# VectorE scales the attention exponentials, GpSimd makes the low halves of the 24 gate chunks, and the heads' low halves come three units later

## The chip, the cores and the metric

One program runs on one core of a Trainium2 chip. The metric is the time of an execution on the device in microseconds (us). The engines named below are TensorE (PE in the rows; PEld is its weight load), VectorE (DVE), ScalarE (ACT), GpSimd (POOL) and SyncE (SP), which issues most of the DMAs. Each engine works through its own queue in order, and the engines meet at semaphores.

## What is computed

The reference is one layer of a hybrid decoder trunk for 512 tokens of width 1024, in float32:

```python
h = rmsnorm(x, norm_mix_pre)
(a_q, a_kc, ..., b_q, ..., c_q, c_k, c_v, mg) = split(h @ w_in)
o_a = nsa_mixer(...)      # 8 heads of 64: compressed, selected and window attention, each with a softmax
o_b = gla_mixer(...)      # chunked gated linear attention
o_c = moba_mixer(...)     # 8 heads of 64: one softmax each
g = sigmoid(mg)           # 3 gates of 1024 channels for each token
merged = g0 * (o_a @ w_branch_a) + g1 * (o_b @ w_branch_b) + g2 * (o_c @ w_branch_c)
x = x + rmsnorm(merged @ w_out)
x = x + rmsnorm((silu(gate) * up) @ w_ffn_out)      # gate, up = split(rmsnorm(x) @ w_ffn_in)
```

In the stretch that is changed two things go on at once: the softmax attention of NSA's selected and window branches and of MoBA, and the products of the normed tokens with the `mg` columns of `w_in` (the gates).

## The kernel before, in words

**Weights.** All weights come from HBM as chunks of 128 x 1024 floats, in a fixed order. SyncE fetches chunk `c` into one of four raw slots (`fetch`, L816). ScalarE makes the high half, a rounded copy, with `hi(c)` (L1026, the activation is L1032). VectorE or GpSimd makes the low half, raw minus high, with a `lo(c)` of its own (VectorE: L1387, instruction L1391; GpSimd: L962, instruction L967). TensorE then takes three matmuls for each product: low x high, high x low, high x high (`three`, lines L2002, L2003, L2004). There are two slots for the halves (`SPLIT_SLOTS`), so `hi(c)` waits until the matmuls of chunk `c - 2` are done. `lo_split` (L371) is the wait for a low half: it picks the semaphore of VectorE or of GpSimd by the chunk's number. Before the change GpSimd makes the chunks from `N_EARLY` to `C_MERGE - 1`, which are those of the input projections, and VectorE makes all others: among them the 24 gate chunks, `C_GATE` to `C_BR - 1`.

**Attention.** It is one loop of 110 steps (`STEPS`), written out on each engine in the same order. A unit is one tile of 128 queries of one pass; there are 24 passes (two for each of the 8 NSA heads, one for each of the 8 MoBA heads) with four units each, 96 in all. The tiles of a pass go 3, 2, 1, 0, so a unit has 512, 384, 256 and 128 keys in turn (causal). In step `u`

- TensorE (`attention_pe`, L745) makes the scores of unit `u` (L761, L762), transposes scaled exponentials for `v = u - 6` (L770; it waits for `s_prob`), multiplies the transposed values of `v = u - 8` with V (L785, L787; it waits for `t_lo`), and then does a quarter of a gate chunk: six matmuls of 512 columns. A gate chunk `f` is used in the steps `4f` to `4f + 3`.
- VectorE (`attention_dve`, L639) adds the bias and takes the row maximum of unit `u` (L654; `s_max`). When `u` is a multiple of 4 it takes the reciprocals of the four row sums of the pass before (L672 for MoBA, L675 and L676 with the NSA gate; `s_rcp`). It makes the low half of the transposed values for `v = u - 7` (L681; `t_lo`), adds the two halves of a finished head (L687; `head_sum`) in steps with `u % 4 == 1`, and makes a gate chunk's low half in steps with `u % 4 == 2`. In the first unit of a head it also writes the far bias of the next head (L510).
- ScalarE (`attention_act`, L548) takes the exponentials of unit `u` with their row sum (L554), the high half of the transposed values for `v = u - 6` (L563), copies half of a finished head (L570) and its high half (L577; `head_hi`), and in steps with `u % 4 == 1` copies the finished gate logits out (L584) and makes the high half of the next gate chunk (L1032).
- GpSimd (L993) multiplies the exponentials of unit `u` in place with the reciprocal (`scale`, L970, instruction L974; `s_prob`), and makes the low half of a finished head (`head_low`, L976, instruction L979; `head_lo`) eight units after the head's last unit.

A head's low half is waited for by ScalarE two heads later (L569) and by TensorE where the branch products start (L725, L737). The first two gate chunks are made ahead of this: `C_GATE` by VectorE in its loop over the projections (L1703), `C_GATE + 1` in step 1 (L658).

Of the kernel before, what the change touches and what calls it, by code (L numbers as in the profile page):

```python
# [22 lines left out]
ALU = mybir.AluOpType  # L23
# [3 lines left out]
P = 128  # L27
# [21 lines left out]
C_MERGE = len(STRAIGHT)  # L49
N_GATES = 3 * KD  # L50
C_GATE = C_MERGE
C_BR = C_GATE + N_GATES
# [18 lines left out]
NX_OF = {k: (j, k - ks[0]) for j, ks in enumerate(NX_K) for k in ks}  # L71
N_FIRST = len(NX_K) + 1
N_EARLY = len(NX_K) + 12
C_POOL = C_MERGE - N_EARLY
FIRST_MOBA = STRAIGHT.index(("cq", 0))
CMP_BACK = FIRST_MOBA + 4

# [45 lines left out]
UNITS = [(br, n, i) for br, n in PASSES for i in TILE_ORDER]  # L123
# [6 lines left out]
def head_units(n):  # L130
    return (8 * n, 8 * n + 7) if n < 8 else (N_NSA + 4 * (n - 8), N_NSA + 4 * (n - 8) + 3)
# [3 lines left out]
LAST_OF = {head_units(n)[1]: n for n in range(N_HEADS)}  # L135
# [19 lines left out]
def count(c):  # L155

    return c - N_SEVEN if c >= C_FOUT else c


def program(nc, wpack, small_d, rows_d, mask_d, x_d, xt_d, pre_d, out_d):  # L160
    ctx = ExitStack()
    with ctx:
        def sem(name):
            return ctx.enter_context(nc.semaphore(name))
# [143 lines left out]
        w_lo_pool, w_lo_dve = sem("w_lo_pool"), sem("w_lo_dve")  # L308
# [35 lines left out]
        s_rcp, s_prob, t_full, pv_done = sem("s_rcp"), sem("s_prob"), sem("t_full"), sem("pv_done")  # L344
# [26 lines left out]
        def lo_split(eng, c):  # L371
            if c < N_EARLY:
                eng.wait_ge(w_lo_dve, c + 1)
            elif c < C_MERGE:
                eng.wait_ge(w_lo_pool, c + 1 - N_EARLY)
            else:
                eng.wait_ge(w_lo_dve, count(c) + 1 - C_POOL)

# [30 lines left out]
        def split_weights(c):  # L409

            return extra.get(c) or (wh[:, c % SPLIT_SLOTS, :], wl[:, c % SPLIT_SLOTS, :])
# [69 lines left out]
        def head_column(n):  # L481

            return 4 * (n % 2) + n // 2 if n < 8 else n
# [14 lines left out]
        def probs(u):  # L498

            i = UNITS[u][2]  # L500
            return sc[:, u // 4 % 3, P_AT[i]:P_AT[i] + P * (i + 1)]

        def stat_of(u, k):
            i = UNITS[u][2]
            return ast[:, u // 4 % 3, k, i:i + 1]

        def far_bias(eng, n):

            h = head_column(n)
            eng.tensor_copy(fullb[:, n % 2, 0:256], small[:, S_FAR + h:S_FAR + h + 1].broadcast_to([P, 256])).then_inc(bias_far, 1)  # L510

        def score_bank(u):
            return bank[u % 2]
# [4 lines left out]
        def output_bank(n):  # L518
            return bank[4 + n % 2]

        def head_rows(n):

            b = 64 * (n % 2)
            o = (oa if n < 8 else oc)[b:b + 64, n % 8 // 2, :, :]
            return tmp[b:b + 64, :], o[:, 0, :], o[:, 1, :]
# [113 lines left out]
        def attention_dve(ve, link, lo, stacked_low):  # L639
            ve.wait_ge(ob_out, 32)  # L640
            ve.wait_ge(near_out, 32)
            for u in range(STEPS):
                if u < len(UNITS):
                    k = UNITS[u][1]
                    n = P * (UNITS[u][2] + 1)
                    ve.wait_ge(s_full, u + 1)
                    if u % 4 == 0 and u >= 12:

                        ve.wait_ge(t_full, u - 8)
                    if u in FIRST_OF:  # L650
                        ve.wait_ge(bias_far, k + 1)
                        ve.wait_ge(band_in[k % 2], 16 * (k // 2 + 1))

                    ve.tensor_tensor_reduce(probs(u), score_bank(u)[:, 0:n], fullb[:, k % 2, 512 - n:512],  # L654
                                            -1.0, 3e38, ALU.add, ALU.min, stat_of(u, 0)).then_inc(s_max, 1)
                    if u == 0:
                        stacked_low(C_MERGE - 1)
                    if u == 1:  # L658
                        lo(C_GATE + 1)
                    if u in FIRST_OF and 1 <= k < N_HEADS - 1:  # L660

                        ve.wait_ge(s_max, u)
                        far_bias(ve, k + 1)
                H = u // 4 - 1
                if u % 4 == 0 and 0 <= H < len(PASSES):
                    br, n = PASSES[H]
                    mine = ast[:, H % 3, :, :]
                    ve.wait_ge(s_exp, 4 * H + 4)
                    if H >= 3:
                        ve.wait_ge(s_prob, 4 * (H - 2))  # L670
                    if br == "m":
                        ve.reciprocal(mine[:, 2, :], mine[:, 1, :]).then_inc(s_rcp, 1)  # L672
                    else:
                        g = 3 * head_column(n) + (1 if br == "s" else 2)
                        link(ve.reciprocal(mine[:, 3, :], mine[:, 1, :]))  # L675
                        ve.tensor_tensor(mine[:, 2, :], mine[:, 3, :], gate[:, :, g], ALU.mult).then_inc(s_rcp, 1)  # L676
                v = u - T_LAG - 1
                if 0 <= v < len(UNITS):
                    n = P * (v % 4 + 1)
                    ve.wait_ge(t_hi, v + 1)  # L680
                    ve.tensor_tensor(ptl[v % 3][:, 0:n], bank[2 + v % 2][:, 0:n], pth[v % 3][:, 0:n].bitcast(F32),  # L681
                                     ALU.subtract).then_inc(t_lo, 1)
                n = LAST_OF.get(u - PV_LAG - 2)
                if n is not None:
                    part = head_rows(n)[0]
                    ve.wait_ge(head_part, n + 1)
                    ve.tensor_tensor(part, output_bank(n)[0:64, :], part, ALU.add).then_inc(head_sum, 1)  # L687
                if u % 4 == 2 and 0 <= u // 4 - 1 < N_GATES + 2:
                    lo(C_GATE + u // 4 + 1)

        def compressed_scores_pe(te, mm):
# [248 lines left out]
        def _(pool):  # L940
# [21 lines left out]
            def lo(c):  # L962
                s, b = c % RAW_SLOTS, c % SPLIT_SLOTS
                n = width_of(c)
                landed(pool, s, c // RAW_SLOTS)
                pool.wait_ge(w_hi, c + 1)
                pool.tensor_tensor(wl[:, b, 0:n], raw[:, s, 0:n], wh[:, b, 0:n].bitcast(F32),  # L967
                                   ALU.subtract).then_inc(w_lo_pool, 1)

            def scale(u):  # L970

                n = P * (UNITS[u][2] + 1)
                pool.wait_ge(s_rcp, u // 4 + 1)
                pool.tensor_tensor(probs(u), probs(u), stat_of(u, 2).broadcast_to([P, n]), ALU.mult).then_inc(s_prob, 1)  # L974

            def head_low(n):  # L976
                part, hi_, lo_ = head_rows(n)
                pool.wait_ge(head_hi, n + 1)
                pool.tensor_tensor(lo_, part, hi_.bitcast(F32), ALU.subtract).then_inc(head_lo, 1)  # L979

            for c in range(C_MERGE):
                if N_EARLY <= c + 2 < C_MERGE:
                    lo(c + 2)
                if c == 6:
                    pool.wait_ge(h_lo, KD)
                    pool.memset(state[:, :, :, :], 0.0).then_inc(const_ready, 1)
                k = c - C_O
                if 0 <= k < NT:
                    pool.wait_ge(o_ms, k + 1)
                    pool.tensor_tensor(stat[:, 32 + 4 * k:36 + 4 * k], stat[:, 16 + 4 * k:20 + 4 * k],  # L990
                                       minus_half[:, 0:4], ALU.pow).then_inc(o_rstd, 1)

            for u in range(len(UNITS) + 8):  # L993
                if u < len(UNITS):
                    scale(u)
                n = LAST_OF.get(u - 8)
                if n is not None:
                    pool.wait_ge(s_prob, min(u + 1, len(UNITS)))
                    head_low(n)
                    pool.wait_ge(head_lo, n + 1)  # L1000
            def y_power(t):
# [350 lines left out]
        def _(ve):  # L1352
# [34 lines left out]
            def lo(c):  # L1387
                high, low = split_weights(c)
                ve.wait_ge(w_hi, count(c) + 1)
                n = width_of(c)  # L1390
                ve.tensor_tensor(low[:, 0:n], raw[:, c % RAW_SLOTS, 0:n], high[:, 0:n].bitcast(F32),  # L1391
                                 ALU.subtract).then_inc(w_lo_dve, 1)
# [120 lines left out]
            for c in range(C_MERGE):  # L1513
# [185 lines left out]
                if c == FIRST_MOBA + 2:  # L1699
                    ve.wait_ge(cmp_ready, 7)  # L1700
                    far_bias(ve, 0)
                    far_bias(ve, 1)
                if c + 2 == C_MERGE:  # L1703
                    lo(c + 2)
            attention_dve(ve, link, lo, stacked_low)

            for s in range(N_GATES):
                n, b = PRODUCTS[s]
# [237 lines left out]
            with ve.Fori(0, 4) as i:  # L1946
                for k in range(4, 8):
                    c = C_FOUT + k
# [48 lines left out]
        def _(te):  # L1997
# [391 lines left out]
            with te.Fori(0, 4) as i:  # L2389
                for k in range(2, 6):  # L2390
                    te.wait_ge(w_hi, i * 4 + count(C_FOUT + k) + 1)
                    te.wait_ge(w_lo_dve, i * 4 + count(C_FOUT + k) + 1 - C_POOL)
                    te.wait_ge(a_hi, i * 4 + k + 1)
# [123 lines left out]
```

## Time and profile before

| | |
|---|---|
| median of 3 runs | 924.05 us (923.48 to 928.54) |
| the profiled execution's own time | 925.45 us |
| its span, first to last instruction | 923.7 us |
| mean granted TensorE clock | 0.997 |
| TensorE busy | 915.4 us (99%) |
| TensorE weight load busy | 806.4 us (87%) |
| VectorE busy | 594.7 us (64%) |
| ScalarE busy | 471.3 us (51%) |
| GpSimd busy | 158.7 us (17%) |
| first and last score matmul of attention | 237.6 us and 452.0 us after the start |

The span is that of the profiled execution; its own time is 1.75 us more, which lies around the span. In the rows below, times are in us from the span's start, "mean ns of one" is an instruction's mean duration, and the idle time at a row's end is that of the engine just before the instruction, with what ended it. Instructions of one engine overlap at their edges: the next one starts some 0.06 us before the one in front of it has ended.

### The profile page before, as it was taken

The page shows a single profiled execution, that of the slowest core. Times are in us where ns is not written, and L with a number is a line of the kernel's source. Part 1 is how long each engine was busy: PE and PEld are TensorE (multiplying, and loading weights), DVE is VectorE, ACT ScalarE, POOL GpSimd, SP SyncE. Part 2 cuts the span into 40 slices and gives each one's busy share as a digit, 9 for nine tenths or more (in the row PEclk, how much of TensorE's full clock was granted, in tenths as well). Part 3 has the DMA queues.
Part 4 walks back from the last instruction along what each step waited for, and adds up shares of the span by engine and source line. Part 5 has one row for each costly group of instructions (what it writes and reads, how often), then busy time and mean ns, then how long its engine had stood idle before and what let it go on. Part 6 is the DMA issues. An engine that isn't in the chain of part 4 may idle for free.

```text
span 923.7 us, 14517 instructions
## 1 busy us (share of the span) xinstructions
PE 915.4 (99%) x5287; PEld 806.4 (87%) x5287; DVE 594.7 (64%) x1146; ACT 471.3 (51%) x912; POOL 158.7 (17%) x168
## 2 busy tenths in 40 slices
PE   9999999999999999999999999999999999999997
PEld 8888888888888888888888888989999999988886
DVE  5998665462555555556667758778888888533335
ACT  6743245333566656676754445255555555323232
POOL 3000263344133334343410001000000000000000
PEclk9999999999999999999999999999999999999999
DMA  9323627222323232464246751122232233232222
GB/s 347 121 71 87 197 92 228 69 92 92 108 81 103 88 102 87 124 246 149 82 170 251 263 166 63 47 92 92 101 128 93 93 110 120 99 107 91 91 91 91
DMA packets 37726, 113.62 MB, mean 123 GB/s; under 512 B 4452, under 2 KB 7076, under 8 KB 36908
## 3 DMA queue, kind: packets, MB, share of 16 engines
q1 hardware_dynamic: 36828, 109.08, 34.7%
q10 hardware_dynamic: 832, 3.67, 1.3%
q8 instruction: 40, 0.66, 0.3%
q14 instruction: 26, 0.21, 0.1%
HBM read 98.87 MB, written 13.66 MB: 122 GB/s over the span
## 4 chain that ended last, share of the span: by engine, by line
PE 98%; DVE 1%; DMA 1%; SPq 0%; issue 0%; ACT 0%; DVEq 0%
PE bank L2002 28%; PE bank L2003 27%; PE bank L2004 27%; PE bank L770 3%; PE bank L762 2%; PE bank L787 2%; PE bank L785 2%; PE bank L761 1%; PE bank L2066 1%; PE bank L2021 1%; DMA xT<-x_features 1%; PE bank L2195 0%; PE bank L2253 0%; PE bank L701 0%; PE bank L2116 0%; PE bank L2182 0%
## 5 line engine op out<-in xcount | busy, mean ns | idle before, releaser
L1032 ACT ACTIVATE w_hi<-w_raw 128x1024 fp32r<-128x1024 f32 (+1 forms) x84 | 88.5, 1054 | 129.1 <-PE bank L2004 125.4
L2002 PE MATMUL bank<-h_hi,w_lo 128*128 128x512 f32 x352 | 140.5, 399 | 0.0
L2003 PE MATMUL bank<-h_lo,w_hi 128*128 128x512 f32 x352 | 138.2, 393 | 0.0
L2004 PE MATMUL bank<-h_hi,w_hi 128*128 128x512 f32 x352 | 138.0, 392 | 0.0
L1391 DVE TENSOR_TENSOR w_lo<-w_raw,w_hi 128x1024 fp32r<-128x1024 f32 (+2 forms) x63 | 77.0, 1223 | 40.7 <-ACT w_hi L1032 40.5
L654 DVE CUSTOM_DVE_ANT_0 sc<-bank,fullb 128x512 f32<-128x512 f32 (+1 forms) x96 | 47.0, 489 | 77.8 <-PE bank L762 76.0
L554 ACT ACTIVATE sc<-sc,ast 128x512 f32<-128x512 f32 (+1 forms) x96 | 53.9, 561 | 72.8 <-DVE ast L654 72.8
L974 POOL TENSOR_TENSOR sc<-sc,ast 128x512 f32<-128x512 f32 (+1 forms) x96 | 66.2, 720 | 130.8 <-DVE ast L676 97.8
L2003 PE MATMUL bank<-tx_lo,op_hi 128*128 128x256 f32 x288 | 81.5, 283 | 0.0
L2004 PE MATMUL bank<-tx_hi,op_hi 128*128 128x256 f32 x288 | 81.5, 283 | 0.0
L2002 PE MATMUL bank<-tx_hi,op_lo 128*128 128x256 f32 x288 | 81.5, 283 | 0.0
L2004 PEld LDWEIGHTS bank<-h_hi,w_hi 128*128 128x128 f32 x352 | 66.5, 189 | 14.6
L2002 PEld LDWEIGHTS bank<-h_hi,w_lo 128*128 128x128 f32 x352 | 66.6, 189 | 11.4
L2003 PEld LDWEIGHTS bank<-h_lo,w_hi 128*128 128x128 f32 x352 | 66.6, 189 | 11.3
L967 POOL TENSOR_TENSOR w_lo<-w_raw,w_hi 128x1024 fp32r<-128x1024 f32 x22 | 52.7, 2397 | 114.7 <-ACT w_hi L1032 114.7
L1834 DVE TENSOR_TENSOR op_lo<-op_sum,op_hi 128x512 fp32r<-128x512 f32 x72 | 49.5, 687 | 20.5 <-ACT op_hi L1270 19.9
L2002 PE MATMUL bank<-w_hi,as_lo 128*128 128x512 f32 x160 | 62.3, 389 | 0.0
L2003 PE MATMUL bank<-w_lo,as_hi 128*128 128x512 f32 x160 | 62.3, 389 | 0.0
L2004 PE MATMUL bank<-w_hi,as_hi 128*128 128x512 f32 x160 | 62.2, 389 | 0.0
L2003 PE MATMUL bank<-h_lo,op_hi 128*128 128x256 f32 x216 | 61.1, 283 | 0.0
L2004 PE MATMUL bank<-h_hi,op_hi 128*128 128x256 f32 x216 | 61.1, 283 | 0.0
L2002 PE MATMUL bank<-h_hi,op_lo 128*128 128x256 f32 x216 | 61.1, 283 | 0.0
(360 smaller groups left out, 2308.8 us busy)
## 6 DMA issues: line engine op xcount, KB each, us to landing
w_raw<-wpack SPq DMA_DIRECT2D x144, 512.0 KB, 3.6
gate_logits<-gl_out SPq DMA_DIRECT2D x24, 256.0 KB, 2.2
gl_in<-gate_logits SPq DMA_DIRECT2D x24, 256.0 KB, 5.3
near_bias<-near_bias ACTq DMA_DIRECT2D x1, 2880.0 KB, 13.4
xT<-x_features SPq DMA_DIRECT2D x8, 256.0 KB, 5.8
xs<-x_in SPq DMA_DIRECT2D x4, 512.0 KB, 8.8
fullb<-near_bias SPq DMA_DIRECT2D x16, 128.0 KB, 2.9
ckx<-cks SPq DMA_DIRECT2D x16, 128.0 KB, 2.8
```

What stands on the lines that cost most here:

```text
L554: sa.activation(probs(u), probs(u), ACT.Exp, bias=stat_of(u, 0), scale=-1.0, accum_out=stat_of(u, 1)).then_inc(s_exp, 1)
L654: ve.tensor_tensor_reduce(probs(u), score_bank(u)[:, 0:n], fullb[:, k % 2, 512 - n:512], -1.0, 3e38, ALU.add, ALU.min, stat_of(u, 0)).then ...
L762: mm(score_bank(u)[:, 0:m], query(n)[:, cols], k1[:, 0:m], start=False, stop=True).then_inc(s_full, 1)
L770: last = te.transpose(bank[2 + v % 2][:, P * (i - j):P * (i - j) + P], sc[:, H % 3, P_AT[i] + P * j:P_AT[i] + P * j + P], ident[:, :])
L967: pool.tensor_tensor(wl[:, b, 0:n], raw[:, s, 0:n], wh[:, b, 0:n].bitcast(F32), ALU.subtract).then_inc(w_lo_pool, 1)
L974: pool.tensor_tensor(probs(u), probs(u), stat_of(u, 2).broadcast_to([P, n]), ALU.mult).then_inc(s_prob, 1)
L1032: sa.activation(split_weights(c)[0][:, 0:n], raw[:, s, 0:n], ACT.Copy).then_inc(w_hi, 1)
L1391: ve.tensor_tensor(low[:, 0:n], raw[:, c % RAW_SLOTS, 0:n], high[:, 0:n].bitcast(F32), ALU.subtract).then_inc(w_lo_dve, 1)
L1834: ve.tensor_tensor(opl[o % RING][:, :], source, oph[o % RING][:, :].bitcast(F32), ALU.subtract).then_inc(op_lo, 1)
L2002: mm(out, ll, rh, start=start, stop=False, skip_group_check=True)
L2003: mm(out, lh, rl, start=False, stop=False, skip_group_check=True)
L2004: return mm(out, lh, rh, start=False, stop=stop, skip_group_check=True)
```

## The change

GpSimd's `scale` goes away. In step `u` VectorE now multiplies the exponentials of unit `u - 4` in place with a `tensor_scalar` whose scalar is a column of one value per partition; it does so after the reciprocals and ahead of the low half of the transposed values. GpSimd makes the low halves of all 24 gate chunks: the first two at the end of its loop over the projections, the others in steps with `u % 4 == 2`, the place that VectorE had for them. VectorE keeps the chunks from `C_BR` on. A head's low half follows on GpSimd 11 units after the head's last unit, in place of 8, right behind a gate chunk's low half and a wait for it. No DMA is added, removed or moved.

```diff
-C_POOL = C_MERGE - N_EARLY
+C_POOL = C_BR - N_EARLY
...
         def lo_split(eng, c):
             if c < N_EARLY:
                 eng.wait_ge(w_lo_dve, c + 1)
-            elif c < C_MERGE:
+            elif c < C_BR:
                 eng.wait_ge(w_lo_pool, c + 1 - N_EARLY)
             else:
                 eng.wait_ge(w_lo_dve, count(c) + 1 - C_POOL)
...
                     if u == 0:
                         stacked_low(C_MERGE - 1)
-                    if u == 1:
-                        lo(C_GATE + 1)
...
                         ve.tensor_tensor(mine[:, 2, :], mine[:, 3, :], gate[:, :, g], ALU.mult).then_inc(s_rcp, 1)
+                v = u - 4
+                if 0 <= v < len(UNITS):
+                    ve.wait_ge(s_rcp, v // 4 + 1)
+                    ve.tensor_scalar(probs(v), probs(v), stat_of(v, 2), None, ALU.mult).then_inc(s_prob, 1)
                 v = u - T_LAG - 1
...
-                if u % 4 == 2 and 0 <= u // 4 - 1 < N_GATES + 2:
+                if u % 4 == 2 and N_GATES <= u // 4 + 1 < N_GATES + 4:
                     lo(C_GATE + u // 4 + 1)
...
-            def scale(u):
-
-                n = P * (UNITS[u][2] + 1)
-                pool.wait_ge(s_rcp, u // 4 + 1)
-                pool.tensor_tensor(probs(u), probs(u), stat_of(u, 2).broadcast_to([P, n]), ALU.mult).then_inc(s_prob, 1)
-
...
             for c in range(C_MERGE):
-                if N_EARLY <= c + 2 < C_MERGE:
+                if N_EARLY <= c + 2:
                     lo(c + 2)
...
-            for u in range(len(UNITS) + 8):
-                if u < len(UNITS):
-                    scale(u)
-                n = LAST_OF.get(u - 8)
+            for u in range(len(UNITS) + 12):
+                if u % 4 == 2 and 2 <= u // 4 + 1 < N_GATES:
+                    lo(C_GATE + u // 4 + 1)
+                n = LAST_OF.get(u - 11)
                 if n is not None:
-                    pool.wait_ge(s_prob, min(u + 1, len(UNITS)))
+                    pool.wait_ge(w_lo_pool, min(C_GATE + u // 4 + 1, C_BR - 1) + 1 - N_EARLY)
                     head_low(n)
                     pool.wait_ge(head_lo, n + 1)
...
-                if c + 2 == C_MERGE:
-                    lo(c + 2)
             attention_dve(ve, link, lo, stacked_low)
```

## Rows read from the trace of the kernel before

**Rows 1.** Page, the chain that ended last, shares of the span by engine.
```profile
PE 98%; DVE 1%; DMA 1%; SPq 0%; issue 0%; ACT 0%; DVEq 0%
```

**Rows 2.** Busy time of one stretch of attention: stretch, length, then each engine's busy us.
```profile
251.50:442.00 190.50, 190.50 (x1044) 164.27 (x1043) 111.74 (x331) 124.41 (x314) 72.48 (x96) 1.00 0.37 121
```

**Rows 3.** Groups by line: count | busy us, mean ns of one | idle before.
```profile
L1391 DVE TENSOR_TENSOR w_lo<-w_raw,w_hi 128x1024 fp32r<-128x1024 f32 x27 | 33.6, 1245 | 15.0 <-ACT w_hi L1032 15.0
...
L681 DVE TENSOR_TENSOR pTl<-bank,pTh 128x384 fp32r<-128x384 f32 x24 | 13.3, 553 | 2.3 <-ACT pTh L563 2.3
...
L681 DVE TENSOR_TENSOR pTl<-bank,pTh 128x128 fp32r<-128x128 f32 x24 | 6.8, 285 | 0.0
...
L974 POOL TENSOR_TENSOR sc<-sc,ast 128x512 f32<-128x512 f32 (+1 forms) x96 | 66.2, 720 | 130.8 <-DVE ast L676 97.8 <-DVE ast L672 33.0
L967 POOL TENSOR_TENSOR w_lo<-w_raw,w_hi 128x1024 fp32r<-128x1024 f32 x22 | 52.7, 2397 | 114.7 <-ACT w_hi L1032 114.7
```

**Rows 4.** Groups by line, VectorE operations with one SBUF input and an SBUF output.
```profile
L1412 DVE COPY rb<-stat 128x512 f32<-128x512 f32 x1 | 0.4, 428 | 0.9 <-POOL stat L960 0.9
...
L1666 DVE TENSOR_SCALAR ghid<-ghid 64x128 f32<-64x128 f32 x1 | 0.2, 220 | 0.0
```

**Rows 5.** Timeline, around gate chunk 7 (kind C): start us, duration us, instruction.
```profile
292.48 0.69 DVE L687 TENSOR_TENSOR tmp<-bank,tmp 64x512 f32<-64x512 f32 x1
...
293.37 0.63 ACT L577 ACTIVATE oa<-tmp 64x512 fp32r<-64x512 f32 x1
...
294.64 1.06 ACT L1032 ACTIVATE w_hi<-w_raw 128x1024 fp32r<-128x1024 f32 x1
...
295.39 0.28 PE L762 MATMUL bank<-ak,aqs 128*128 128x128 f32 x1
...
295.74 1.23 DVE L1391 TENSOR_TENSOR w_lo<-w_raw,w_hi 128x1024 fp32r<-128x1024 f32 x1 [0.99 <-ACT w_hi L1032]
...
298.29 0.19 PEld L785 LDWEIGHTS bank<-pTh,av 128*128 128x128 f32 x1
...
298.51 0.19 PEld L2002 LDWEIGHTS bank<-h_hi,w_lo 128*128 128x128 f32 x1
```

**Rows 6.** Timeline, high halves of gate chunks 5, 22 (kind B) and 23 (C), chunk 5's use.
```profile
275.74 1.05 ACT L1032 ACTIVATE w_hi<-w_raw 128x1024 fp32r<-128x1024 f32 x1
...
280.02 0.19 PEld L2002 LDWEIGHTS bank<-h_hi,w_lo 128*128 128x128 f32 x1
...
432.59 1.05 ACT L1032 ACTIVATE w_hi<-w_raw 128x1024 fp32r<-128x1024 f32 x1
...
442.13 1.06 ACT L1032 ACTIVATE w_hi<-w_raw 128x1024 fp32r<-128x1024 f32 x1
```

**Rows 7.** Timeline, GpSimd behind ScalarE in the projections.
```profile
227.00 1.06 ACT L1032 ACTIVATE w_hi<-w_raw 128x1024 fp32r<-128x1024 f32 x1 [3.28 <-PE bank L2004]
...
228.20 2.39 POOL L967 TENSOR_TENSOR w_lo<-w_raw,w_hi 128x1024 fp32r<-128x1024 f32 x1 [3.04 <-ACT w_hi L1032]
```

**Rows 8.** Timeline, a small VectorE operation with and without a low half on GpSimd.
```profile
125.88 0.17 DVE L1641 TENSOR_SCALAR stat<-stat 128x4 f32<-128x4 f32 x1
...
127.11 2.37 POOL L967 TENSOR_TENSOR w_lo<-w_raw,w_hi 128x1024 fp32r<-128x1024 f32 x1
...
128.93 0.57 DVE L1641 TENSOR_SCALAR stat<-stat 128x4 f32<-128x4 f32 x1
```

**Rows 9.** Timeline, gate chunk 2 early in attention.
```profile
248.56 1.05 ACT L1032 ACTIVATE w_hi<-w_raw 128x1024 fp32r<-128x1024 f32 x1
...
252.16 0.30 PE L785 MATMUL bank<-pTh,av 128*128 128x128 f32 x1
```

**Rows 10.** Timeline, a MoBA head's first unit behind chunk 19 (kind C).
```profile
405.60 1.06 ACT L1032 ACTIVATE w_hi<-w_raw 128x1024 fp32r<-128x1024 f32 x1
...
409.85 0.29 DVE L510 COPY fullb<-small 128x256 f32<-128x256 f32 x1
...
411.66 0.36 PE L785 MATMUL bank<-pTh,cv 128*128 128x256 f32 x1
```

## The prediction

> **What bounds the kernel now.** I read the chain that ended last first: 98% of it is TensorE [rows 1]. Then the busy time by stretch: over 190.5 us of attention TensorE is busy for 190.50 us, at a granted clock of 1.00, while VectorE has 111.74 us of work, ScalarE 124.41 and GpSimd 72.48 [rows 2]. The list of waits has none of TensorE's inside attention. So nothing that the change takes off VectorE, ScalarE or GpSimd can make attention shorter: the steps already follow each other at TensorE's own pace. What is left to ask is whether one of the changed results comes later than TensorE asks for it. For that I read the timeline, gate chunk by gate chunk.
>
> **The change part by part.**
>
> *Scales leave GpSimd.* 96 instructions of 720 ns, 69.1 us, all beside TensorE's work [rows 3]; gain 0.
>
> *Low halves come to GpSimd.* 24 of 2.397 us, 57.5 us, in place of 24 of 1.245 us (29.9 us) on VectorE [rows 3]. GpSimd's load falls by 11.6 us, but each low half is ready later. GpSimd starts 0.14 us after the high half's end (227.00 + 1.06 = 228.06, start 228.20) [rows 7], VectorE 0.04 us after it [rows 5].
>
> *Scales come to VectorE.* No row shows this operation with a column as its scalar. The nearest, one SBUF input and an SBUF output, take 220 ns for 128 elements and 428 ns for 512 [rows 4], so 0.54 ns an element: 0.22, 0.29, 0.36 and 0.43 us, 1.30 for a pass and 31.1 us in all, against the 29.9 that leave. The lower bound is these; the upper is one element a cycle, 285 ns for 128 and 553 for 384 [rows 3]. I take the lower. VectorE is 59% busy in this stretch, so the sum costs nothing; its place in the queue can. The Trainium skill ("VectorE: DVE Perf Modes", section on the TRN2 errata) gives 58 cycles plus half the elements at 0.96 GHz. An estimate by it is 0.26 us for 384 elements; the rows of this case say 0.36, and the sum would stay at its size by either.
>
> *What stands behind a scale on VectorE.* In steps with u % 4 == 1 the scale of 384 stands ahead of L681 and of L687, which come 0.30 us later (0.36 less the overlap of 0.06). In the passes in which a head ends, ScalarE's L577 waits for L687. L687 then ends at 292.48 + 0.69 + 0.30 = 293.47, L577 starts at 293.52 in place of 293.37 [rows 5], and the high half behind it on ScalarE comes 0.15 us later.
>
> *When the low halves are ready.* The 24 chunks fall in three kinds. A (9 chunks, no head ends) has over 1.2 us in hand. B (chunks 5, 9, 13, 17, 20, 22; first and last high half in [rows 6]): 275.74 + 1.05 + 0.15 + 0.14 + 2.40 = 279.48, and TensorE loads it at 280.02: 0.54 us in hand. C (chunks 7, 11, 15, 19, 21, 23; first in [rows 5], last in [rows 6]): 294.64 + 1.06 + 0.15 + 0.14 + 2.40 = 298.39, loaded at 298.51: 0.12 us in hand. So the gate matmuls just don't wait.
>
> *The shared access.* L1641, 128 x 4, takes 0.17 us by itself; where a low half is running on GpSimd it takes 0.57 and ends at 129.50, while the low half ends at 129.48 [rows 8]. VectorE was held until GpSimd's instruction was over. The new scale is an operation of this kind, and the 128-wide one (u % 4 == 3) falls into GpSimd's low half. Behind it in VectorE's queue stands L681 for 128 elements, for which TensorE's L785 waits in the next step. It would end 0.31 us behind GpSimd's low half (0.03 + 0.28).
> The Trainium skill ("Advanced Engine Details and Errata", VectorE Performance Modes) says that two-port VectorE instructions and GpSimd's block each other. Rows 8 show VectorE's side alone. An estimate by the other side: GpSimd's low half would start up to 0.2 us later in kind C, and the gates would wait some 0.1 us there, 0.6 us in all.
>
> - A: over 0.9 us in hand, 0.
> - B: 279.48 + 0.31 = 279.79, needed at 280.02 - 0.22 = 279.80; with 0.05 for the semaphore, 0.05 us each, 0.3 us.
> - C: it is a race. VectorE's L654 can start at 295.39 + 0.28 = 295.67 and the scale 0.21 later, at 295.88; GpSimd starts at 294.64 + 1.06 + 0.15 + 0.14 = 295.99. If VectorE is in first, 0. If GpSimd is, L681 ends at 298.70 and is needed at 298.29 [rows 5]: 0.4 us each. Bounds 0 and 2.4 us; the two starts are within 0.11 us, so I take half, 1.2.
> - Chunk 2, before the pipeline is full: 248.56 + 1.05 + 0.14 + 2.40 + 0.31 = 252.46, needed at 252.13 [rows 9]: 0.35 us once.
>
> *Heads' low halves.* They move behind a gate chunk's low half, so to 409.45 to 410.74 in [rows 10] (405.60 + 1.06 + 0.15 + 0.14 + 2.40, and 0.1 for the wait on its own semaphore). Those who wait for them do so two heads later, or, for the last head, behind a high half whose time doesn't move: 0. But VectorE's L510 (409.85) is of the held kind too. Held to 410.87, with the reciprocal, the scale of 512 and L681 for 256 behind it, VectorE is ready near 411.8, and L785 wants it at 411.66: 0.2 us in the three MoBA chunks of kind C, 0.6 us, less what has been lost there already (0.3). In NSA's passes the reciprocals' product is held so, with 0.04 us or nothing at the end.
>
> *Queues.* SyncE's fetch of chunk c + 4 waits for chunk c's low half, four steps after it is made; nothing moves. TensorE's waits keep their number.
>
> Sum: 0.3 + 1.2 + 0.35 + 0.3 = 2.15, rounded to 2.0 us longer. The profiled execution has 925.45 us; so 927.45 against it. The median of the runs is 1.40 us below it: 924.05 + 2.0 = 926.0 us, +0.2%. About 0.5% (4.6 us) is what a measurement of this kernel can tell from no change.
>
> **The rivals.**
>
> *Nothing moves.* VectorE wins every race and the 0.05 us are not there: 924 us. For it: TensorE's steps have the same length to a few ns from pass to pass. Against it: chunk 2's margin is negative by my rows.
>
> *The hold goes on through the head's low half.* Slower than before clearly. In the 12 passes of kinds B and C GpSimd has the head's low half (1.29 us) right behind the chunk's. If VectorE's waiting scale doesn't get in between, L681 for 128 is late by a further 1.39 us: B 1.4 us, C 1.8, so 6 x 1.4 + 6 x 1.8 = 19 us, 943 us. It decides in the gap between the two GpSimd instructions. Against it: GpSimd waits there for its own semaphore, and in rows 8 VectorE went on within 0.02 us.
>
> *Scale at one element a cycle.* Then it isn't of the two-port kind and (as the reductions beside GpSimd in the trace) isn't held; but L687 is 0.5 us later, the high half 0.35, and the gates of kind C wait 0.1 to 0.2 us: 925 us.
>
> *A gain.* It would need a wait of TensorE that the profile doesn't show. A faster VectorE frees ScalarE's exponentials by 0.1 to 1 us in steps with u % 4 == 3, but TensorE asks for them two steps later.
>
> **How the numbers follow.** The forecast (waits of some tenths in few passes, +0.5 to +4 us) 0.60; nothing moves 0.16; one element a cycle 0.06; held through both 0.09; more stalls of the forecast's kind than I counted, over 4.6 us, 0.06; a gain over 0.5% 0.03. Slower by over 0.5%: 0.09 + 0.06 = 0.15, with a little of the forecast's tail 0.17. Faster 0.03. The rest, 0.80, is within 0.5%. The range starts at 923.3, a little under no change, and ends at 930, where all races are lost (+3.9) and two tenths more are lost in each pass of kind B or C.
>
> **What would show it.** Right: TensorE's waits in attention name L681 and are under 0.5 us each; TENSOR_SCALAR of 128 elements shows a mean near 1 us with an end at the end of GpSimd's L967, while that of 256 and 512 stays at 0.29 and 0.43; L967 has 46 instructions of 2.4 us. Wrong: idle of TensorE before L2002 by L967 (the low half itself is late), scales held over L979, or attention's length unchanged to 0.1 us.

## The result, and the profile after

The changed kernel takes 932.66 us (median of 7 runs, 930.68 to 934.01), against 924.16 us for the kernel before (median of 7, 923.48 to 928.54): 1.0086 times as long, with an interval of 1.0072 to 1.0099. So it is slower by 0.9%, outside the range of the prediction. The profiled execution of after took 932.66 us with a span of 930.9 us, 7.2 us more than the span of before. Both have the same mean granted clock (0.997).

The page of after: busy times, the chain that ended last, and two groups.

```profile
PE 918.7 (99%) x5287; PEld 805.2 (86%) x5287; DVE 630.0 (68%) x1218; ACT 471.5 (51%) x912; POOL 150.2 (16%) x96
...
PE 95%; DVE 2%; issue 1%; DMA 1%; SPq 0%; ACT 0%; DVEq 0%
...
L969 POOL TENSOR_TENSOR w_lo<-w_raw,w_hi 128x1024 fp32r<-128x1024 f32 x46 | 110.5, 2402 | 263.9 <-ACT w_hi L1028 263.9
...
L678 DVE TENSOR_SCALAR sc<-sc,ast 128x512 f32<-128x512 f32 (+1 forms) x96 | 66.1, 688 | 0.9
```

TensorE's share of the chain is 95%, where it was 98% [rows 1]. The low halves on GpSimd are what was forecast, 46 of 2.4 us. The scales on VectorE (L678) are not: 66.1 us in place of the 31.1 of the prediction, 688 ns each. The windows show where the time went (stretch, length, then the busy us of TensorE, its weight load, VectorE, ScalarE and GpSimd, the granted clock, and DMA), the stretch of [rows 2] in after:

```profile
251.50:442.00 190.50, 187.11 (x1008) 157.36 (x1007) 139.82 (x380) 120.07 (x302) 61.19 (x31) 1.00 0.36 118
```

TensorE was busy for all of these 190.50 us before; now it is idle for 3.39 us of them, at the same granted clock. (The ends of matmuls are modelled, so part of a wait can lie inside a busy time; the lengths of the steps, below, show all of it.) The groups by shape, in attention alone, say which scale is dear:

```profile
L678 DVE TENSOR_SCALAR sc<-sc,ast 128x128 f32<-128x128 f32 x24 | 34.4, 1435 | 0.0
...
L678 DVE TENSOR_SCALAR sc<-sc,ast 128x512 f32<-128x512 f32 x24 | 12.2, 510 | 0.8
...
L678 DVE TENSOR_SCALAR sc<-sc,ast 128x384 f32<-128x384 f32 x24 | 10.0, 417 | 0.0
L678 DVE TENSOR_SCALAR sc<-sc,ast 128x256 f32<-128x256 f32 x24 | 9.4, 391 | 0.0
```

The smallest takes longest: 1435 ns on average. It is the one that falls into GpSimd's low half; in 19 of the 24 passes it is held, for 1.33 to 2.47 us, and in five it takes 0.28. And the waits of TensorE in attention (from 237 to 480 us; us in total, times, longest), of which before had none there:

```profile
PEld bank L772 <- DVE sc L678: 7.1, 10, 0.9
...
PE bank L772 <- DVE pTl L683: 3.5, 7, 0.5
...
PEld bank L772 <- issue: 2.9, 11, 0.6
```

All stand at L772, the transposes, and not at the product with V (L787), where the prediction had looked. (One wait can stand both at the weight load and at the matmul, so the rows don't add up. The first names the scale, L678, which is not what they wait for. The transposes of step u ask for the scale of unit u - 6 and for the low half of unit u - 8. In the step of chunk 7 below, the scale that they ask for, of 256, had ended at 295.45, 4 us earlier; what they lack is the low half, L683.)

**Step by step.** Attention's first 95 steps, each taken from its first score matmul to that of the next, add up to 6.71 us more than in before. Attention starts 0.18 us earlier than in before, and 0.70 us more come behind the last score matmul: 0.63 of them are one more wait at the transposes (459.29, 0.80 us behind that matmul, where before has 0.17), behind a scale of 256 that a head's low half holds for 1.33 us. By the prediction's terms:

| place | measured, us | forecast, us |
|---|---|---|
| chunk 2 | 0.69 | 0.35 |
| kind B (chunks 5, 9, 13, 17; 20 and 22 nothing) | 0.26, 0.32, 0.28, 0.27 | 0.3 for six |
| kind C in NSA, u % 4 == 0 (chunks 7, 11, 15) | 0.69, 0.71, 0.66 | 1.2 for all six |
| kind C in MoBA, u % 4 == 1 (chunks 19, 21, 23) | 0.74, 0.71, 0.25 | 0.3 |
| first passes of seven NSA heads, u % 4 == 1 | 0.10 to 0.13 each, 0.82 in all | 0 |
| all other steps | 0.3 | 0 |

Chunk 7 shows the mechanism, in the timeline of after (start, duration, instruction):

```profile
295.72 1.06 ACT L1028 ACTIVATE w_hi<-w_raw 128x1024 fp32r<-128x1024 f32 x1
...
296.43 0.28 PE L764 MATMUL bank<-ak,aqs 128*128 128x128 f32 x1
...
296.92 2.41 POOL L969 TENSOR_TENSOR w_lo<-w_raw,w_hi 128x1024 fp32r<-128x1024 f32 x1 [8.19 <-ACT w_hi L1028]
...
296.96 2.45 DVE L678 TENSOR_SCALAR sc<-sc,ast 128x128 f32<-128x128 f32 x1
...
298.64 0.39 PE L763 MATMUL bank<-ak,aqs 128*128 128x512 f32 x1
...
299.33 0.28 DVE L683 TENSOR_TENSOR pTl<-bank,pTh 128x128 fp32r<-128x128 f32 x1
299.40 1.28 POOL L975 TENSOR_TENSOR oa<-tmp,oa 64x512 fp32r<-64x512 f32 x1
...
299.72 0.31 PEld L772 LDWEIGHTS bank<-ident,sc 128*128 128x128 f32 x3 [0.89 <-DVE sc L678]
299.75 0.52 PE L772 MATMUL bank<-ident,sc 128*128 128x128 f32 x3 [0.49 <-DVE pTl L683]
...
300.34 0.36 DVE L674 TENSOR_TENSOR ast<-ast,gate 128x4 f32<-128x4 f32 x1
...
301.72 0.34 PE L763 MATMUL bank<-ak,aqs 128*128 128x384 f32 x1
```

GpSimd is in first by 0.04 us. VectorE's scale of 128 then takes 2.45 us in place of 0.28 and ends at 299.41, 0.08 us behind GpSimd's end at 299.33. L683 behind it is done at 299.61, and TensorE's transposes have waited for it: the step from 298.64 to 301.72 is 3.08 us long. In before the same step takes 2.39 us, from 297.61 to 300.00, and its deadline stands in these rows of the timeline:

```profile
297.61 0.39 PE L761 MATMUL bank<-ak,aqs 128*128 128x512 f32 x1
...
298.07 0.49 PE L770 MATMUL bank<-ident,sc 128*128 128x128 f32 x3
...
298.29 0.19 PEld L785 LDWEIGHTS bank<-pTh,av 128*128 128x128 f32 x1
...
300.00 0.33 PE L761 MATMUL bank<-ak,aqs 128*128 128x384 f32 x1
```

The transposes of unit u - 6 overwrite the bank that was read for the low half of unit u - 8, so they wait for the same value of `t_lo` as the product with V of unit u - 8, and they stand ahead of it in TensorE's queue, 0.22 us earlier (298.29 - 298.07), or 0.36 us in steps with u % 4 == 1.

In MoBA VectorE wins the race (chunk 19, after), and pays later:

```profile
411.62 0.28 DVE L678 TENSOR_SCALAR sc<-sc,ast 128x128 f32<-128x128 f32 x1
411.68 2.48 POOL L969 TENSOR_TENSOR w_lo<-w_raw,w_hi 128x1024 fp32r<-128x1024 f32 x1 [8.21 <-ACT w_hi L1028]
...
414.23 1.30 POOL L975 TENSOR_TENSOR oa<-tmp,oa 64x512 fp32r<-64x512 f32 x1
...
414.57 1.11 DVE L510 COPY fullb<-small 128x256 f32<-128x256 f32 x1
...
415.80 0.49 DVE L678 TENSOR_SCALAR sc<-sc,ast 128x512 f32<-128x512 f32 x1
...
416.20 0.42 DVE L683 TENSOR_TENSOR pTl<-bank,pTh 128x256 fp32r<-128x256 f32 x1
...
416.76 0.63 PE L772 MATMUL bank<-ident,sc 128*128 128x128 f32 x4 [0.54 <-DVE pTl L683]
```

The far bias of the next head (L510, 0.29 us before [rows 10]) is held by the head's low half that the change puts here. With the reciprocal and the scale of 512 behind it, L683 is late for TensorE by 0.54 us.

### The profile page after: what moved, and what is told of

It reads as the page before. It is cut to its first block, busy times and chain, and to the rows that moved or that the text cites. A ratio compares the mean times of both kernels' runs of the same rounds, so it can differ in the third digit from the quotient of the medians.

```text
span 930.9 us, 14528 instructions
## 1 busy us (share of the span) xinstructions
PE 918.7 (99%) x5287; PEld 805.2 (86%) x5287; DVE 630.0 (68%) x1218; ACT 471.5 (51%) x912; POOL 150.2 (16%) x96
## 4 chain that ended last, share of the span: by engine, by line
PE 95%; DVE 2%; issue 1%; DMA 1%; SPq 0%; ACT 0%; DVEq 0%
PE bank L1996 27%; PE bank L1998 27%; PE bank L1997 27%; PE bank L772 3%; PE bank L789 2%; PE bank L764 2%; PE bank L787 1%; PE bank L2060 1%; PE bank L763 1%; PE bank L2015 1%; DMA xT<-x_features 1%; PE bank L2189 0%; DVE sc L678 0%; PE bank L2247 0%; PE bank L703 0%
## 5 line engine op out<-in xcount | busy, mean ns | idle before, releaser
L1028 ACT ACTIVATE w_hi<-w_raw 128x1024 fp32r<-128x1024 f32 (+1 forms) x84 | 88.4, 1054 | 129.3 <-PE bank L1998 125.7
L969 POOL TENSOR_TENSOR w_lo<-w_raw,w_hi 128x1024 fp32r<-128x1024 f32 x46 | 110.5, 2402 | 263.9 <-ACT w_hi L1028 263.9
L1996 PE MATMUL bank<-h_hi,w_lo 128*128 128x512 f32 x352 | 140.7, 400 | 0.0
L654 DVE CUSTOM_DVE_ANT_0 sc<-bank,fullb 128x512 f32<-128x512 f32 (+1 forms) x96 | 47.1, 490 | 60.1 <-PE bank L764 56.6
L1996 PE MATMUL bank<-tx_hi,op_lo 128*128 128x256 f32 x288 | 81.5, 283 | 0.0
L1996 PEld LDWEIGHTS bank<-h_hi,w_lo 128*128 128x128 f32 x352 | 66.6, 189 | 11.4
L1387 DVE TENSOR_TENSOR w_lo<-w_raw,w_hi 128x1024 fp32r<-128x1024 f32 (+2 forms) x39 | 47.6, 1221 | 29.9 <-ACT w_hi L1028 29.5
L678 DVE TENSOR_SCALAR sc<-sc,ast 128x512 f32<-128x512 f32 (+1 forms) x96 | 66.1, 688 | 0.9
L1996 PE MATMUL bank<-w_hi,as_lo 128*128 128x512 f32 x160 | 62.3, 389 | 0.0
L1996 PE MATMUL bank<-h_hi,op_lo 128*128 128x256 f32 x216 | 61.1, 283 | 0.0
```

Of the source, the lines that this page charges most:

```text
L678: ve.tensor_scalar(probs(v), probs(v), stat_of(v, 2), None, ALU.mult).then_inc(s_prob, 1)
L1028: sa.activation(split_weights(c)[0][:, 0:n], raw[:, s, 0:n], ACT.Copy).then_inc(w_hi, 1)
L1996: mm(out, ll, rh, start=start, stop=False, skip_group_check=True)
```

## The experiments

Line numbers move by a few between the kernels: the waits of TensorE below are always at its transposes. Each kernel is set against runs of the kernel before on the same chip; the sums "in attention" are taken step by step against before, as above.

**The scale behind the transposed low half.**

```diff
-                v = u - 4
-                if 0 <= v < len(UNITS):
-                    ve.wait_ge(s_rcp, v // 4 + 1)
-                    ve.tensor_scalar(probs(v), probs(v), stat_of(v, 2), None, ALU.mult).then_inc(s_prob, 1)
                 v = u - T_LAG - 1
...
                                      ALU.subtract).then_inc(t_lo, 1)
+                v = u - 4
+                if 0 <= v < len(UNITS):
+                    ve.wait_ge(s_rcp, v // 4 + 1)
+                    ve.tensor_scalar(probs(v), probs(v), stat_of(v, 2), None, ALU.mult).then_inc(s_prob, 1)
```

> The changed kernel with two lines of VectorE's queue exchanged: in every step the low half of the transposed values comes first, the scale second. Same work on every engine. Theory H (GpSimd's low half holds VectorE's two-port scale, and what stands behind the scale comes late): TensorE waits for the low half of the transposed values, which now stands ahead of the held scale, while the scale itself is asked for two steps later. So the waits of 0.26 to 0.71 us in the steps with u % 4 == 0 (4.1 us in all) vanish, and most of those of 0.1 to 0.74 in the steps with u % 4 == 1 (2.4 us) with them: 925 to 927 us; the 128-wide scales still last 1.4 us on average. Rival L (VectorE simply has more to do than its slack allows, scales of 0.28 to 0.49 us being dearer than forecast): its work is the same, so it stays late in sum, and the time stays at 930 us or more.

Measured: 924.39 us, 1.0000 times before (0.9990 to 1.0009); 0.31 us more in attention, all of it in two steps behind chunks 19 and 21. The whole 8 us are gone although the scale of 128 takes as long as before the exchange, 1422 ns on average where after has 1435. The time is 0.6 us below what was expected. The group by shape and the timeline at chunk 7:

```profile
L684 DVE TENSOR_SCALAR sc<-sc,ast 128x128 f32<-128x128 f32 x24 | 34.1, 1422 | 0.0
```

```profile
294.21 2.40 POOL L969 TENSOR_TENSOR w_lo<-w_raw,w_hi 128x1024 fp32r<-128x1024 f32 x1 [8.11 <-ACT w_hi L1028]
294.76 0.29 DVE L679 TENSOR_TENSOR pTl<-bank,pTh 128x128 fp32r<-128x128 f32 x1 [0.54 <-ACT pTh L563]
294.97 1.74 DVE L684 TENSOR_SCALAR sc<-sc,ast 128x128 f32<-128x128 f32 x1
...
296.28 0.49 PE L772 MATMUL bank<-ident,sc 128*128 128x128 f32 x3
```

The scale is held as before, to 296.71. But the low half of the transposed values (L679), which reads a PSUM bank, runs beside GpSimd in its 0.29 us and is done at 295.05, 1.2 us before TensorE asks for it. So what costs time is not the hold by itself, nor VectorE's load, but what is queued behind the scale, held or not.

**The scales alone** (low halves of the gate chunks stay on VectorE; heads' low halves after 11 units, without the wait for a gate chunk).

```diff
-C_POOL = C_BR - N_EARLY
+C_POOL = C_MERGE - N_EARLY
...
+                    if u == 1:
+                        lo(C_GATE + 1)
...
-                if u % 4 == 2 and 2 <= u // 4 + 1 < N_GATES:
-                    lo(C_GATE + u // 4 + 1)
```

> Only the scales move to VectorE; VectorE keeps the low halves of the gate chunks, and GpSimd has only the heads' low halves, 11 units behind a head. H: nothing long runs on GpSimd any more, so the 128-wide scale lasts 0.28 us; the heads' low halves run right behind ScalarE's high half and can hold the 256-wide scale of that step by up to 1.2 us, with the 512-wide low half of the transposed values behind it: up to 0.5 us in each of 12 passes that end a head. 925 to 931 us, with no wait in the steps u % 4 == 0 in which no head's low half runs. L: VectorE has 30 us more work in attention than in the changed kernel, so it is later everywhere: over 935 us.

Measured: 929.26 us, 1.0054 (1.0037 to 1.0071); 3.63 us in attention. The scale of 128 has 282 ns now, with no low half beside it. But 2.69 us come in four steps (u = 19, 35, 51, 67; 0.64 to 0.70 each), not in twelve passes as expected: at the other heads' low halves in attention VectorE's scale of 256 is in first. Timeline at u = 18 and 19:

```profile
273.68 1.28 POOL L977 TENSOR_TENSOR oa<-tmp,oa 64x512 fp32r<-64x512 f32 x1 [45.09 <-ACT oa L577]
...
273.76 1.36 DVE L680 TENSOR_SCALAR sc<-sc,ast 128x256 f32<-128x256 f32 x1
...
275.04 0.68 DVE L685 TENSOR_TENSOR pTl<-bank,pTh 128x512 fp32r<-128x512 f32 x1
...
275.87 0.41 PE L774 MATMUL bank<-ident,sc 128*128 128x128 f32 x2 [0.50 <-DVE pTl L685]
```

It is the same mechanism at another place: the head's low half now starts as soon as its high half is there, in the step whose scale is 256 wide, and holds that one. Another 1.04 us are in the first passes of the NSA heads (eight steps, 0.09 to 0.15 each; all other steps together are 0.1 us shorter), where GpSimd has nothing to do: there the queue is just too long for TensorE's transposes, as the reciprocals' product and the scale of 512 stand ahead of the low half.

**The low halves alone** (GpSimd keeps the scales, and takes the gate chunks too: four scales at the start of a pass, then the low half).

```diff
-                    ve.tensor_scalar(probs(v), probs(v), stat_of(v, 2), None, ALU.mult).then_inc(s_prob, 1)
...
+                if u % 4 == 0 and 4 <= u <= len(UNITS):
+                    for v in range(u - 4, u):
+                        scale(v)
                 if u % 4 == 2 and 2 <= u // 4 + 1 < N_GATES:
                     lo(C_GATE + u // 4 + 1)
...
+                    pool.wait_ge(s_prob, min(4 * (u // 4), len(UNITS)))
                     head_low(n)
```

> Only the low halves move: GpSimd makes the gate chunks' low halves and also scales, as it did before (four scales of a pass in a row, ahead of the next chunk's low half). VectorE has less work than in either kernel. H: VectorE has no two-port scale to be held; the far-bias copy can still be held by a head's low half, and the scales of a pass come behind that, 1 us later than before, with over 1 us in hand: 924 to 926 us. L: the same, 924 to 925. A third theory, that the GpSimd low halves themselves are late for the gate matmuls: waits in front of the gate matmuls in the kind-C chunks, 925 to 929.

Measured: 924.11 us, 1.0002 (0.9991 to 1.0012), and in attention 0.00 us: every step has its length of before, with 24 low halves of 2.4 us on GpSimd. So the low halves themselves are not late for the gates; they do harm only through what they hold.

**Heads' low halves back at 8 units.**

```diff
-            for u in range(len(UNITS) + 12):
+            for u in range(len(UNITS) + 8):
...
-                n = LAST_OF.get(u - 11)
+                n = LAST_OF.get(u - 8)
```

> The changed kernel with the third part undone: heads' low halves 8 units behind the head, so in GpSimd's queue ahead of the gate chunk's low half instead of behind it. H: the copy and the 512-wide scale in the steps u % 4 == 0 of the next pass are no longer held (the 2.4 us of waits in steps u % 4 == 1 vanish), but the head's low half (1.29 us) now runs while the 256-wide scale of step u % 4 == 2 wants the port: it is held by some 1.1 us, the low half of the transposed values behind it ends 0.65 us too late, in the 12 passes in which a head ends: +7.8 - 2.4, 936 to 939 us. L: GpSimd's order does not matter to VectorE: 932 to 933 us.

Measured: 932.16 us, 1.0084 (1.0067 to 1.0101); 7.48 us in attention. The three dear MoBA steps are gone (0.69 us are left in steps with u % 4 == 1, where after has 2.44), and the same four steps as with the scales alone come in, 0.70 to 0.74 each, 2.81 in all. The steps with u % 4 == 0 stay at 3.85 us in sum (4.06 in after), but not in place: chunks 5, 9, 13 and 17 now cost nothing, and chunks 20 and 22 cost 0.41 and 0.47. The 256-wide scales in this kernel:

```profile
L678 DVE TENSOR_SCALAR sc<-sc,ast 128x256 f32<-128x256 f32 x24 | 12.7, 530 | 0.0
```

I had expected twelve of these 24 to be held, and 936 to 939 us; four are, for 1.41 to 1.45 us, and the others take 0.35. Elsewhere VectorE is in first. The "three units later" of the change is therefore worth little by itself, 0.77 us in attention (7.48 against 6.71) and nothing in the medians: it trades one held instruction for another.

**The gate chunk's low half in two instructions of 512 columns.**

```diff
+                if c >= C_GATE:
+                    pool.tensor_tensor(wl[:, b, 0:512], raw[:, s, 0:512], wh[:, b, 0:512].bitcast(F32), ALU.subtract)
+                    pool.tensor_tensor(wl[:, b, 512:n], raw[:, s, 512:n], wh[:, b, 512:n].bitcast(F32),
+                                       ALU.subtract).then_inc(w_lo_pool, 1)
...
```

> The changed kernel, but GpSimd makes each gate chunk's low half in two instructions of 512 columns, back to back, with no semaphore between them. H with a grant between two GpSimd instructions: the held 128-wide scale lasts at most about 1.4 us (mean near 0.8 in place of 1.43) and the waits of 0.26 to 0.71 us in the steps u % 4 == 0 vanish; the two halves end some 0.2 us later than one instruction, so some kind-C gate matmuls may wait 0.2 us: 928 to 930 us. If VectorE is held through back-to-back instructions: scale mean 1.6 us and more, 933 to 936 us. L: no change, 932.

Measured: 931.68 us, 1.0090 (1.0073 to 1.0107); 5.07 us in attention. For the steps that the edit aims at the expectation holds: the scale of 128 falls to 749 ns, and 4.06 us at u % 4 == 0 become 0.52. VectorE gets in between two GpSimd instructions that stand back to back, with no semaphore between them. The total misses, since VectorE is now early for the next GpSimd instruction, the head's low half (timeline, chunk 7):

```profile
297.01 1.29 POOL L980 TENSOR_TENSOR oa<-tmp,oa 64x512 fp32r<-64x512 f32 x1
...
297.63 0.70 DVE L674 TENSOR_TENSOR ast<-ast,gate 128x4 f32<-128x4 f32 x1
...
299.33 0.52 PE L772 MATMUL bank<-ident,sc 128*128 128x128 f32 x3 [0.28 <-DVE pTl L683]
```

The product of 128 x 4, 0.17 us by itself, is held for 0.70, and the step with u % 4 == 1 pays 0.47 to 0.50 us in chunks 7, 11 and 15. The two dearest steps of MoBA stay (0.71 and 0.73).

**A constant in place of the column.** (This kernel leaves the normalisation of the exponentials out. Its instructions and waits are otherwise the same.)

```diff
-                    ve.tensor_scalar(probs(v), probs(v), stat_of(v, 2), None, ALU.mult).then_inc(s_prob, 1)
+                    ve.tensor_scalar(probs(v), probs(v), 0.5, None, ALU.mult).then_inc(s_prob, 1)
```

> The changed kernel with the scale's per-partition column replaced by the constant 0.5 (so the exponentials are not normalised; the waits are the same). It prices the column: if it costs the extra 0.06 us, the scales not held last 0.22, 0.29, 0.36 and 0.43 us, as the nearest rows of before had it, in place of 0.28, 0.35, 0.42 and 0.49. TensorE's waits then shrink by some 0.06 us each, 24 of them: 1 to 2 us less than the changed kernel.

Measured in one run: 931.26 us, 5.74 us in attention. The groups by shape:

```profile
L678 DVE TENSOR_SCALAR sc<-sc 128x128 f32<-128x128 f32 x24 | 34.1, 1420 | 0.0
...
L678 DVE TENSOR_SCALAR sc<-sc 128x384 f32<-128x384 f32 x24 | 8.5, 355 | 0.0
```

The 384-wide scale, which nothing holds, takes 355 ns with a constant and 417 ns with a column: 0.06 us is the price of the column. The held one doesn't change. The extra time in the first passes of the seven NSA heads falls from 0.82 us to 0.44 (0.05 to 0.09 each). In all, attention takes 0.97 us less than in after.

**Only the scales of 128, and only those of 512, behind the low half.** The edit of the first experiment for `v % 4 == 3` alone, and then for `v % 4 == 0` alone. The first of the two:

```diff
-                if 0 <= v < len(UNITS):
+                if 0 <= v < len(UNITS) and v % 4 < 3:
...
+                if 0 <= v < len(UNITS) and v % 4 == 3:
```

> The changed kernel; of the four scales of a pass only the 128-wide one (step u % 4 == 3, the one that GpSimd's low half of the gate chunk holds) goes behind the low half of the transposed values. H: the 4.1 us of waits in steps u % 4 == 0 vanish; those in steps u % 4 == 1 (2.4 us: copy and 512-wide scale) stay, or grow where VectorE no longer loses time before: 927.5 to 929.5 us. L: the order of one short scale changes the work of no step, 931 us or more.

> The changed kernel; only the 512-wide scale (step u % 4 == 0, beside the far-bias copy and the reciprocals) goes behind the low half of the transposed values. The 2.4 us of waits in steps u % 4 == 1 vanish, but for up to 0.2 us where the copy is held by a head's low half; the 4.1 us in steps u % 4 == 0 stay: 929 to 931 us. Together with the run before, the two parts are to add up to the whole of the first experiment. Of the 2.4 us the part in front of which no GpSimd instruction runs (0.1 us in each of 8 NSA heads' first passes, about 1 us) is plain queue length: the scale of 0.49 us in front of the low half of the transposed values.

Measured: 929.25 us (1.0062, 1.0045 to 1.0079) with the 128 behind: all of u % 4 == 0 is gone (4.06 to 0.00), and u % 4 == 1 costs 3.71. With the 512 behind, 927.61 us (1.0042, 1.0026 to 1.0059), below the 929 to 931 that were expected: u % 4 == 1 is all but gone (2.44 to 0.30), and u % 4 == 0 costs 3.23 in place of staying at 4.06. There chunks 5, 9, 13 and 17 cost 0.40 or 0.41 each, chunks 20 and 22 0.36 and 0.38, and the race of kind C in NSA goes the other way and costs nothing (timeline, chunk 7):

```profile
295.30 0.28 DVE L678 TENSOR_SCALAR sc<-sc,ast 128x128 f32<-128x128 f32 x1
295.37 2.46 POOL L973 TENSOR_TENSOR w_lo<-w_raw,w_hi 128x1024 fp32r<-128x1024 f32 x1 [8.20 <-ACT w_hi L1032]
```

A shift of some hundredths of a microsecond makes an instruction 0.28 or 2.45 us long. The two parts do not add up to the whole, as I had expected them to: they give back 2.89 and 2.97 us in attention, 5.86 together, and the first experiment, which has all four scales behind, gives back 6.40. What one of them takes away in one step comes up in part in another, as the 3.71 in place of 2.44 shows. I found no version that beats before: in before TensorE never waits in attention, and two kernels (1.0000 and 1.0002) just reach that.

## Why the prediction was wrong

**Right.** That nothing could be gained, since TensorE bounds attention. That only the place in the queue counts, and that the 128-wide scale is held to the end of GpSimd's low half, with the low half of the transposed values behind it: the waits name it. The first undoing (1.0000) shows that the place of the scale ahead of the low half is the whole cost. The count of lost races came out too, three of six chunks of kind C, but by luck: half was put for want of a reason to choose, and the races did not fall by chance. All three in NSA were lost and all three in MoBA won. The rival in which the hold goes on through the head's low half fell: in the timeline of chunk 7 VectorE's scale ends at 299.41, and GpSimd's next instruction begins at 299.40, not ahead of it. VectorE gets in even between back-to-back instructions (the low half in two). The low halves are in time for the gates (the low halves alone: 0.00 us).

**The step that failed** is the deadline. The prediction said that "TensorE's L785 waits in the next step" for the low half of the transposed values, and took 298.29, 279.80, 252.13 and 411.66 as the times at which it is needed: the loads or products with V. But the transposes (L770) ahead of it wait for the same semaphore value. In the timeline of before they stand at 298.07, 279.58, 251.92 and 411.30: 0.22 us earlier, 0.36 us where u % 4 == 1. The forecast's own times against the right deadline: kind C 298.70 - 298.07 = 0.63 (0.69 measured), kind B 0.05 + 0.22 = 0.27 (0.26 to 0.32), MoBA 0.2 + 0.36 = 0.56 (0.74 and 0.71), chunk 2 0.35 + 0.22 = 0.57 (0.69). And a term that was set at 0 appears, the first passes, where the queue's length alone makes the low half late. What came lies nearest to the branch that had a chance of 0.06, more stalls of the forecast's kind than were counted: in kind B they were four in place of six, but longer, and the first passes came on top. Two of the signs of being right failed with it: waits under 0.5 us each (a step grew by up to 0.74) and a scale of 128 near 1 us (1.435).

**Sizes.** The column makes each scale 0.06 us dearer than the rows without one said: unheld 0.28, 0.35, 0.42 and 0.49 us in place of 0.22, 0.29, 0.36 and 0.43. The constant's 0.355 us for 384 elements is what the rows of before gave. The prediction's estimate by the Trainium skill ("VectorE: DVE Perf Modes", section on the TRN2 errata), 0.26 us, took the 58 cycles of its table; the same section adds that this gives too little and that the fixed part was measured at about 150 cycles. An estimate with 150 is 0.36 us, and the measurement agrees with that. In the first passes the column makes nearly half of the extra time (0.82 us with it, 0.44 without). For kind C the prediction took half of the races at 0.4 us, 1.2 us; it was three at 0.69, 2.05 us. In MoBA the prediction took 0.3 off for "what has been lost there already"; nothing had been, as VectorE had won the race there. Against the forecast's 2.15 us that makes, from the table, 0.34 (chunk 2), 0.83 (B), 0.85 (C in NSA), 1.4 (MoBA), 0.82 (first passes) and 0.3 (rest) more: 6.7 us. The upper end of the range doesn't follow from these terms either: with all races lost they make 0.3 + 2.4 + 0.35 + 0.3 = 3.35 us, or 3.65 with the 0.6 of MoBA in full, not 3.9.

**The race itself.** The prediction had VectorE's scale at 295.88 and GpSimd at 295.99, as the high half was to come 0.15 us later. It came 0.04 us later (the start of L1028 is 0.71 us ahead of the score matmul of 128, where it was 0.75), and VectorE's scale 0.04 us later than put. GpSimd won by 0.04. The 0.14 us from the high half's end to the low half's start held (296.78 to 296.92). In chunk 19 VectorE is as quick (0.22 us from the start of L654 to that of the scale in both chunks), but the low half starts 0.28 us behind that of L654 (411.40 to 411.68) where it is 0.18 in chunk 7 (296.74 to 296.92). What makes NSA and MoBA differ there was not tested.

**The Trainium skill's rule** that two-port VectorE instructions and GpSimd's block each other ("Advanced Engine Details and Errata", VectorE Performance Modes) agrees with the runs on VectorE's side, and weakly on GpSimd's: where a scale of VectorE was running, GpSimd's low half took 2.41 to 2.48 us in place of 2.39 to 2.41, though at 411.68 the scale had another 0.22 us to go, and a head's low half took 1.38 in place of 1.29 (heads' low halves back at 8 units, chunk 7). The profile's spans of GpSimd are rough, so how long GpSimd waits is not shown. The forecast by that side, gates waiting 0.1 us in kind C, did not come: inside attention there is no wait of TensorE at the gate matmuls (L1996).

## What to carry to other kernels

Look for the first instruction of the waiting engine that asks for a semaphore value, not for the one that uses the data: a buffer that is given back can be asked for earlier than the data in it, and the profile of a kernel without waits names neither. Where a wait has several semaphores, look up what each of them waits for: the profile may name the wrong one. On VectorE, put an operation with SBUF operands that may fall beside a GpSimd instruction behind whatever the bounding engine waits for; here two statements in the other order are worth all of 8 us. And a margin of a few hundredths of a microsecond before such a hold can't be counted on: price it at what it costs when lost.

## What the hardware showed that was not expected

The hold has a plain size: it lasts to the end of the GpSimd instruction that is running, whatever is queued behind that one, and a little more that grows with the width. The 128-wide scale ends 0.08 us behind GpSimd's end, the product of 128 x 4 0.03 (298.33 against 298.30 in the kernel with two halves), the copy of 256 0.15 (415.68 against 415.53 at chunk 19), and the one held scale of 512 (452.83 to 453.86 in after) 0.28. So a 128-wide scale of 0.28 us took up to 2.47 us beside a low half of 2.41, and a product of 128 x 4 took 0.70 in place of 0.17. Subtractions that read PSUM were not held at all.

The clock may have a small part in the medians. Both profiled executions have one stretch ahead of attention at a lower granted clock, with TensorE busy throughout; windows of before, then of after:

```profile
170.00:180.00 10.00, 10.00 (x55) 8.70 (x54) 6.89 (x13) 2.24 (x3) 2.36 (x1) 0.83 0.31 107
```

```profile
170.00:180.00 10.00, 10.00 (x55) 8.71 (x54) 7.08 (x13) 2.24 (x3) 2.36 (x1) 0.83 0.34 107
```

The 0.83 is 3.4 us (174.5 to 177.9) at a granted clock of 0.50, the lower of the two levels (1.2 GHz), and the rest at the upper (2.4 GHz). Of the experiments' profiles the one with the constant has this stretch too. In the other seven the clock is 1.00 there, and attention starts 1.4 to 2.0 us earlier (237.6 us in before, 235.8 with the first experiment). A mean clock of 0.998 or less was seen in 18 of the 46 runs with a clock on record of the three kernels that take 924 us, and in 21 of 27 of the six timed kernels in which TensorE waits. At a clock of 0.999, one run of after has 930.68 us and those of before lie near 923.5: 7.2 us, as in the profiles; the medians differ by 8.5. The gap is widest for the kernel with two halves: 5.07 us in attention, 7.95 between the medians. Where the clock is lower in the runs without a profile, and whether the waits bring it about, stays open.
